# A padded pitch for the stationary operands of a split-precision block kernel

## The reference

```python
# first block
h = rmsnorm(x, g_pre);  proj = h @ w_in            # 2048 x 18464
o_a = gated_delta(...)                             # 16 heads of 128, chunks of 64
y_a = (rmsnorm(o_a) * silu(z_a)) @ w_br_a
y_b = (silu(layernorm(conv31(glu))) * silu(z_b)) @ w_br_b
mixed = (gate_a * y_a + gate_b * y_b) @ w_out
x = x + rmsnorm(mixed);  e = p @ w_ple_proj
x = x + rmsnorm(sigmoid(x @ w_ple_gate) * e)
# second block
proj = rmsnorm(x) @ w_in_2                         # latents, gates, a 3-tap convolution
q, kv = rmsnorm(q_a) @ w_q_b, rmsnorm(c_kv) @ w_kv_b
y_mla = (causal_attention(q, kv) * silu(z_mla)) @ w_o_mla
y_conv = (b_gate * conv3(c_gate * c_in) * silu(z_conv)) @ w_o_conv
out = (sigmoid(g_mla) * y_mla + sigmoid(g_conv) * y_conv) @ w_out_2
x = x + rmsnorm(out)
```

## Time and profile before

| | |
|---|---|
| median of 3 runs | 2660.43 us (2659.6 to 2660.44) |
| the profiled execution's own time | 2659.6 us |
| its span, first to last instruction | 2659.6 us |
| PE busy | 2545.2 us (96%) |
| PEld busy | 2110.4 us (79%) |
| DVE, ACT, POOL busy | 1654.2 us (62%), 1162.3 us (44%), 170.6 us (6%) |
| mean granted TensorE clock | 0.987 of full speed |

### The profile page before, as it was taken

The page is one execution under the profiler, slowest core; times in us unless marked ns, Lnnn a source line. Parts: engine busy times, 40 slices in busy tenths (PEclk is TensorE's granted clock), DMA queues, the critical chain, the costliest instruction groups (busy, mean ns, idle before and its releaser), DMA issues.

```text
span 2659.6 us, 32737 instructions
## 1 busy us (share of the span) xinstructions
PE 2545.2 (96%) x12351; PEld 2110.4 (79%) x12351; DVE 1654.2 (62%) x2127; ACT 1162.3 (44%) x1484; POOL 170.6 (6%) x244
## 2 busy tenths in 40 slices
PE   4999999988999999999999889999999999999997
PEld 3878888877879878888887767787787788888886
DVE  3699998678576666745645554555464544455554
ACT  4444444445352533424445454344444444443443
POOL 2000000153000100101000010000000000000000
PEclk9999999989999999999999999999999999999999
DMA  4666666444333333637665554555554655675563
GB/s 141 203 190 225 201 213 198 158 159 161 109 128 107 116 127 101 210 134 269 227 204 174 166 174 145 180 181 176 179 196 159 209 187 188 197 263 197 181 222 111
DMA packets 225973, 469.66 MB, mean 177 GB/s; under 512 B 12062, under 2 KB 12119, under 8 KB 224663
## 3 DMA queue, kind: packets, MB, share of 16 engines
q1 hardware_dynamic: 213098, 418.57, 47.4%
q0 software_dynamic: 12768, 49.59, 5.5%
HBM read 445.05 MB, written 23.07 MB: 176 GB/s over the span
## 4 chain that ended last, share of the span: by engine, by line
PE 69%; DVE 3%; ACT 2%; issue 1%; DMA 1%; POOL 0%; DVEq 0%; ACTq 0%; POOLq 0%
PE acc L1997 58%; PE aux L2125 4%; PE aux L2027 1%; DVE w_lo L1305 1%; PE aux L2391 1%; PE aux L2390 1%; PE aux L2130 1%; PE aux L2206 1%; PE aux L2210 0%; DVE cy L1519 0%; ACT w_hi L763 0%; PE aux L2195 0%; PE aux L2205 0%; PE acc L2297 0%; DMA r1l<-delta_branch_spill 0%
## 5 line engine op out<-in xcount | busy, mean ns | idle before, releaser
L1305 DVE TENSOR_TENSOR w_lo<-raw,w_hi 128x1024 fp32r<-128x1024 f32 (+1 forms) x790 | 975.4, 1238 | 852.2 <-ACT w_hi L763 841.7
L763 ACT CAST w_hi<-raw 128x1024 fp32r<-128x1024 f32 (+1 forms) x790 | 827.6, 1051 | 1295.7 <-PE acc L1997 1274.3
L1997 PE MATMUL acc<-w_hi,r1h 128*128 128x512 f32 (+1 forms) x1920 | 764.1, 398 | 17.6 <-issue 10.1
L1997 PE MATMUL acc<-w_hi,r1l 128*128 128x512 f32 (+1 forms) x1920 | 749.0, 390 | 0.0
L1997 PE MATMUL acc<-w_lo,r1h 128*128 128x512 f32 (+1 forms) x1920 | 748.7, 390 | 0.0
L1997 PE MATMUL acc<-w_hi,r2h 128*128 128x512 f32 x1216 | 484.9, 399 | 2.1 <-DVE w_lo L1305 1.8
L1997 PE MATMUL acc<-w_hi,r2l 128*128 128x512 f32 x1216 | 481.2, 396 | 0.0
L1997 PE MATMUL acc<-w_lo,r2h 128*128 128x512 f32 x1216 | 481.2, 396 | 0.0
L1997 PEld LDWEIGHTS acc<-w_hi,r1h 128*128 128x128 f32 x1920 | 363.8, 189 | 92.9 <-issue 15.5
L1997 PEld LDWEIGHTS acc<-w_hi,r1l 128*128 128x128 f32 x1920 | 363.0, 189 | 75.4
L1997 PEld LDWEIGHTS acc<-w_lo,r1h 128*128 128x128 f32 x1920 | 363.8, 189 | 70.0 <-issue 1.0
(11 more groups left out here) (426 smaller groups left out, 1634.8 us busy)
## 6 DMA issues: line engine op xcount, KB each, us to landing
raw<-in_w_in SPq DMA_DIRECT2D x264, 1024.0 KB, 5.0
raw<-in_w_out SPq DMA_DIRECT2D x32, 1024.0 KB, 5.0
raw<-in_w_br_b SPq DMA_DIRECT2D x16, 1024.0 KB, 5.2
raw<-in_w_br_a SPq DMA_DIRECT2D x16, 1024.0 KB, 6.7
raw<-in_w_ple_gate SPq DMA_DIRECT2D x16, 1024.0 KB, 5.1
raw<-in_w_o_mla SPq DMA_DIRECT2D x16, 1024.0 KB, 5.1
raw<-in_w_o_conv SPq DMA_DIRECT2D x16, 1024.0 KB, 5.1
raw<-in_w_q_b SPq DMA_DIRECT2D x8, 1024.0 KB, 5.1
```

Source lines behind the costliest of these rows:

```text
L763: nc.scalar.copy(w_hi[:, h % HL, 0:n], raw[:, k % RAW, x * HALF:x * HALF + n]).then_inc(hi_ready, 1)
L1305: V.tensor_tensor(w_lo[:, h % HL, 0:n], raw[:, k % RAW, x * HALF:x * HALF + n], w_hi[:, h % HL, 0:n].bitcast(F32), ALU.subtract).then_inc( ...
L1997: ins = T.matmul(acc[:, s, x, 0:n], a[:, kt0 + k, xs_], w[:, h % HL, at], start=start and k == 0 and m == 0, stop=stop and k == kts - 1 an ...
```

## The change

Each of the 16 channel tiles of `r1h`, `r1l`, `r2h` and `r2l` takes up 260 elements (1040 bytes) of a partition in place of 256 (1024 bytes); the last four of each are not used. Each of the four tensors grows by 256 bytes. `OWN_BYTES` is smaller by 1024, so that `delta_at` moves by 512 bytes down in all, and what lies behind `r2l` stays where it was. With the tiles no longer contiguous, the DMAs of `reload` and of the spill to `cT_dram` are written with the channel tile as a dimension of its own (runs of 1 KB in SBUF in place of 4 KB), and so is ACT's copy of `c3`.

```diff
-OWN_BYTES = 50 * 1024
+OWN_BYTES = 50 * 1024 - 1024
+PITCH = TOK + 4
...
-        r1h, r1l = sb("r1h", [P, KT, TOK], F32R), sb("r1l", [P, KT, TOK], F32R)
+        r1h, r1l = [sb(n, [P, KT, PITCH], F32R)[:, :, 0:TOK] for n in ("r1h", "r1l")]
...
-        tail_at = delta_at + 2 * KT * TOK * 4
+        tail_at = delta_at + 2 * KT * PITCH * 4
...
-            r2h, r2l = s1("r2h", [P, KT, TOK], F32R), s1("r2l", [P, KT, TOK], F32R)
+            r2h, r2l = [s1(n, [P, KT, PITCH], F32R)[:, :, 0:TOK] for n in ("r2h", "r2l")]
...
-                    pool.dma_start(r[:, CT * q:CT * (q + 1), :].rearrange("p a b -> p (a b)"), src[n, q]).then_inc(sem(f"operand_landed{q}"), 16)
+                    pool.dma_start(r[:, CT * q:CT * (q + 1), :], src[n, q].rearrange("p (a b) -> p a b", a=CT)).then_inc(sem(f"operand_landed{q}"), 16)
...
-                    pool.dma_start(cT_dram[n, bass.ds(i, 1)].rearrange("a p n -> p (a n)"),
-                                   r[:, 2 * CT:3 * CT].rearrange("p a b -> p (a b)")).then_inc(sem("cT_out"), 16)
+                    pool.dma_start(cT_dram[n, bass.ds(i, 1)].rearrange("a p (k b) -> p (a k) b", k=CT),
+                                   r[:, 2 * CT:3 * CT]).then_inc(sem("cT_out"), 16)
...
-                sig(nc.scalar.copy(r1h[:, 2 * CT:3 * CT].rearrange("p a b -> p (a b)"), c3[:].rearrange("p a b -> p (a b)")), "c_hi", i + 1)
+                sig(nc.scalar.copy(r1h[:, 2 * CT:3 * CT], c3[:]), "c_hi", i + 1)
```

## The result

The changed kernel takes 2668.19 us (median of 6 runs, 2665.52 to 2672.38) against 2660.01 us for the one before (6 runs, 2658.71 to 2661.41). The ratio is 1.0032, with a 95% interval of 1.0021 to 1.0042: slower by 8.2 us. The profiled execution took 2668.21 us, its span is 2666.4 us.

The account below looks back on a forecast made before the run. The prediction took PE's stream of 9,408 `gemm` matmuls to bound the kernel. On 2659.6 us it put +22.7 us of stream, -2 hidden and +2 for DMAs: 2682.3, predicted as 2683 us, range 2652 to 2716 us.

Parts of the forecast that it names:

- the sum on the stream: `gemm`'s matmuls on PE: changed distances between starts add 9.6 - 6.1 + 19.2 = +22.7 us.
- what hides: PE's waits that slower matmuls use up, in the first round of QKVZ: -2 us.
- the DMAs: Reloads and spills with 512 runs of 1 KB, exposed at YA's last quarter: +2 us (0.0 to 3.5).
- The step that failed: `gemm`'s loads: any start off a 64-byte boundary costs the same, so 16 and 48 run at 233.3 ns.
- the odd offsets: Tiles at 16 and 48 modulo 64, half of either set: +19.2 us for `r1`, 0 for `r2`.
- The quarter of the tiles that I had at 0: Tiles starting at 0 modulo 64 in `r1` and `r2`: claimed to run at 226.7 ns.
- the wait in QKVZ: First round of QKVZ: PE's 10.8 us wait for DVE's convolution absorbs slower `r1` matmuls, -2 us.
- The 54 us of waits: PE's waits for other engines without the first 24.1 us: some 54 us, so little can hide.
- the region: Rival: `r2` is slower for lying above byte 131,072, offsets do nothing; 2662 us, chance 0.14.
- dearer odd offsets: Rival: tiles at 16 and 48 modulo 64 cost more than 32; up to +54.1 us, 2715 us, chance 0.15.
- Between: Rival: odd offsets at 230 ns, cost growing with distance to the next 64-byte boundary; +7.0 us, 2668 us, chance 0.12.
- a conflict on the side of the gain: Rival: odd offsets avoid a load's conflict with the moving stream; 2654 us (chance 0.08) or 2591 us (0.09).

Follow-up runs that it names:

- e1: The kernel before with `r2`, and what shares its arena from `delta_at` on, 32 bytes lower: 2635.82 us, ratio 0.9907.
- e2: The kernel before with 128 bytes of padding ahead of `raw`, so that everything moves by 128 bytes: 2659.75 us, one run.
- e3: The kernel before with the moving operands and `raw` moved by 128 bytes, `r1` and `r2` by 256: 2684.39 us, one run.
- e5: The kernel before with the pitch of 1040 bytes for `r1` alone: 2677.11 us, ratio 1.0068.
- e4: The kernel before with high and low parts of each channel tile interleaved, the change's DMA forms without its offsets: 2660.19 us, ratio 1.0003.
- e6: The kernel before with the pitch of 1040 bytes for `r2` alone: 2651.59 us, ratio 0.9972.
- e8: e1 with all of `r2` one element, 4 bytes, further on: 2657.03 us, one run.
- e7: e1 with all of `r2` 16 bytes further on: 2651.38 us, one run.

## Why the prediction was wrong

The direction was right, and so was where to look; the size and the rule behind it were not. The forecast was +22.7 us, 2677 to 2688 us as its own range; the measured +8.2 us lie inside the wide range and far below that. Of the 14.5 us between the two, the sum on the stream makes up 6.7, what hides 5 and the DMAs 2. By its steps:

- **That PE's stream bounds the kernel and that the stationary operand's address costs time in it: right.** e1 moves one set of operands by 32 bytes and the kernel by 25 us. The estimate for a full swing, 6.6 ns times 3,648 matmuls or 24 us, was met. The rule of the Trainium skill's page "SBUF — State Buffer", section "Specifications (TRN2)", lines of 16 bytes, does not cover this: 32 bytes are whole lines, and they cost 25 us. That of the Trainium skill's page "TensorE: Matmul & The Clock Gate", section "Part 2: What happens when you issue a matmul", independent ports for the two operands, does not either: e2 and e3 show that the cost depends on where the two lie to each other.
- **The step that failed** is the one that carried the odd offsets: "what counts is whether the 512 bytes of a load start on a 64-byte boundary". It read 0 and 32 modulo 64 off two points, and both points fit another rule as well, which I had not written down: distance from the moving operand modulo 256, 0 for `r1` and 32 for `r2`. In its place the runs showed that distance: in the changed kernel the tiles at 0 modulo 64 are not spared (tile 4 of `r1`, at distance 64, averages 232.5 ns), those within 16 bytes of distance 0 are nearly so, and e3 slows all of `r1`, which stays at 0 modulo 64, to 232.4 ns. I noted that the moving stream always starts at a multiple of 64 and did not set the two addresses side by side.
- **The terms.** Worked out from the distances that stand in both traces, `gemm`'s stream grew by 23.1 us for `r1` (forecast +28.8) and shrank by 7.1 us for `r2` (forecast -6.1): +16.0 us for the forecast +22.7. The quarter of the tiles that I had at 0 is not spared as such; tiles 0, 1 and 15 of `r1` are for the most part, and tiles 13 to 15 of `r2` (226.7 to 229.0 ns on average), and a few more come out at about 230 ns. The averages are 231.5 and 231.3 ns, beside the 231.7 that I forecast for both. That nearness is luck: the rule behind it was not the right one. What made `r1`'s term too large is what I multiplied: `r1` averaged 227.1 ns before, not 226.7, as the first matmuls behind an interruption are slower, and 8% of its matmuls are of 256 columns or stand beside an interruption and are not in this count.
- **What hides.** I took -2 us for the wait in QKVZ. It was some -7 us: from the first matmul of a phase to that of the next, GLU grew by 2.0 us where its stream grew by 5.0, GT3 shrank by 0.3 where it grew by 0.8, and QKVZ grew by 2.7 where it grew by 5.4. e5 gives back the same in the same phases, and e3 too, where GLU's stream grew by 6.2 us: as a wait does that is used up. QKVZ's part is the least certain: in the seven kernels with `r1` at distance 0 it took 584.3 to 586.2 us. For GLU and GT3 it is the transposes of `u` and the matmuls behind them that show it: before, PE waited 1.2 us for DVE ahead of the transposes and 2.3 us for `w_lo`, in e5 not at all and 0.6 us. That is 2.9 of the 4.1 us. Groups of PE in 98:410, before and in e5:

```profile
L1997 PE MATMUL acc<-w_hi,r1h 128*128 128x512 f32 x446 | 174.4, 391 | 2.4 <-DVE w_lo L1305 2.3
...
L2027 PE MATMUL aux<-ident,u 128*128 128x128 f32 x32 | 4.3, 278 | 1.2 <-DVE u L1328 1.2
```

```profile
L1998 PE MATMUL acc<-w_hi,r1h 128*128 128x512 f32 x443 | 174.8, 395 | 0.6 <-DVE w_lo L1306 0.6
...
L2028 PE MATMUL aux<-ident,u 128*128 128x128 f32 x32 | 4.1, 272 | 0.0
```

- **The DMAs: +2 us forecast, nothing measured** (e4: -0.1% to +0.1%, which is -2 to +3 us). POOL's issue grew by 0.2 us, at the lower end of my estimate, and 512 runs take it no longer than 256 did for `xres`. The wait for the last quarter of YA, on which the +2 us hung, was 0.7 us in the one profiled execution of the kernel before and is absent in those of all nine other kernels, with long or short runs.
- **The 54 us of waits.** The "some 54 us" of waits for other engines hold 10.1 us that the view puts down to "issue" and to no engine. No term of the sum hangs on it.
- **The single execution.** The spans differ by 6.8 us, the streams and waits inside the phases by 10.7 us. The rest is ahead of them: the first matmul of `gemm` starts at 51.6 us before and at 47.8 after. Of these 3.8 us, 1.2 are shorter waits for `crow` and `xt`, and the others go with the granted clock, which was 0.83 in 30:50 of the kernel before, 1.00 in the changed one, and 0.83 or 0.91 in all eight experiments. As e5 and e6, which hold the change between them, have 0.91 and 0.83, I take it for chance; no run shows its cause. In QA it goes the other way. The first matmuls behind PE's wait of 7.3 us for `mix`, the changed kernel:

```profile
1536.00:1538.00 2.00, 1.74 (x5) 0.50 0.00 0
1538.00:1541.00 3.00, 3.00 (x14) 0.99 0.35 70
```

  At 1.2 GHz for some 2 us; before, the same stretch had 0.83. By the starts this is some +2 us of the changed kernel's QA, found in e3 and e6 as well and not in the others.

So the rivals: the region is refuted (e1), as are dearer odd offsets (the worst average of any tile is 233.7 ns). "Between" had the right time, 2668 us, but as a rule, a cost growing with the distance to the next 64-byte boundary, it is refuted too (tile 4 of `r1`). A dependence on the moving stream, which I named as a conflict on the side of the gain, is what e2 and e3 show; it took away on one side and gave on the other. Open is how the hardware makes it and whether it is a conflict at all, why its period is 256 bytes, and whether the 13.3 ns that are left above 213.3 can go: no offset tried here went below 226.7 ns.

## What to carry to other kernels

Where PE streams float32r matmuls of 512 columns with a load each, note the address of the stationary operand relative to the moving one's, modulo 256, and put them at the same place. It costs a few bytes of padding and was worth 0.9% here, while 4, 16 or 32 bytes off cost up to 3% of every matmul. Read it off the distance between starts: durations do not show it. And when two points suggest a rule about an address, list all the rules that fit both, the other operand's address among them, before working out a sum from one.

## What the runs showed of the hardware

- The distance of two streamed matmuls of 512 columns is 226.7 ns (32 cycles over 512 at 2.4 GHz) with the operands 0 apart modulo 256, and in streams with one other relation of the addresses 232.4 ns (4 bytes, e8; 128 bytes, e3) and 233.3 ns (32 bytes, the kernel before; 160, e3). In the changed kernel, where the relation changes with the tile, the averages by tile run from 226.7 to 233.7 ns. Single distances are not even: 225 to 238 ns in its YM, in a pattern that repeats from block to block, and 228 to 241 ns in e3's.
- Behind an interruption the first dozen distances of a stream at 0 average up to 231 ns, then it is 226.7 (e1).
- At 16 bytes apart two steady states exist, 226.7 and 233.3 ns, each kept until the stream is interrupted (e7).
- The plain float32 matmuls of 128 columns of the delta rule kept their 112 ns in e1, where of one pair, `kb` and `bf`, only the second moved by 32 bytes. In e2 and e3 their operands kept their places to each other, so these say nothing on it.
- POOL's issue of a DMA takes 0.53 to 0.57 us with 128 runs of 4 KB (kernel before) and 0.71 to 0.79 us with 512 of 1 KB (changed kernel); `xres`, with 256 of 2 KB, takes 0.74.
